# Four quarter-unit subtractions of a Trainium2 decoder kernel, moved from VectorE to GpSimd

## The reference

```python
for i in range(DEPTH):
    h = rms_norm(x, norm_w[i])
    y = nsa_mixer(h, ...) if i % 2 == 0 else hgrn2_mixer(h, ...)
    x = x + y
return rms_norm(x, final_norm)
```

```python
q_raw, f_raw, i_in, z = split(h @ w_in)        # w_in is 1024 x 4096
q = silu(q_raw);  f = lb + (1 - lb) * sigmoid(f_raw);  k = 1 - f
o = recurrence(q, k, log f, i_in)              # 8 heads of 128 x 128 state, decay f
y = (rms_norm_per_head(o) * g_norm * silu(z)) @ w_out
```

## Time and profile before

| | |
|---|---|
| median of 3 runs | 322.13 us (322.1 to 322.6) |
| the profiled execution, whole | 321.99 us |
| its span in the profile | 320.2 us |
| PE busy | 308.6 us, 96% of the span |
| DVE busy | 241.7 us, 75% |
| ACT busy | 183.2 us, 57% |
| POOL busy | 47.2 us, 15% |
| granted TensorE clock | 0.998 of full speed |

### The profile page before, as it was taken

One profiled execution on the slowest core, in us unless ns is written; L12 is line 12 of the kernel. 1 busy time (PEld: TensorE's weight loads), 2 busy tenths in 40 slices (PEclk: granted clock), 3 DMA queues, 4 the chain that ended last, 5 costly groups with the idle time before them and its releaser, 6 DMA issues.

```text
span 320.2 us, 5858 instructions
## 1 busy us (share of the span) xinstructions
PE 308.6 (96%) x2232; PEld 262.3 (82%) x2232; DVE 241.7 (75%) x424; ACT 183.2 (57%) x387; POOL 47.2 (15%) x50
## 2 busy tenths in 40 slices
PE   7999999998999999999999999999999989999992
PEld 4789788866889988887678889999997768889882
DVE  4878987679979888998848825397778997498823
ACT  5886047354794596667446823867273207897423
POOL 1003011031123253446000100000000201103000
PEclk9999999999999999999999999999999999999999
DMA  7999999960192900051270983465914234001011
GB/s 239 394 355 204 259 371 203 313 256 0 41 213 55 211 11 2 0 194 70 66 266 0 333 314 79 186 206 188 332 64 183 81 122 146 3 0 66 2 66 66
DMA packets 28683, 49.33 MB, mean 154 GB/s; under 512 B 3240, under 2 KB 7600, under 8 KB 28656
## 3 DMA queue, kind: packets, MB, share of 16 engines
q1 hardware_dynamic: 25760, 44.30, 44.8%
q10 hardware_dynamic: 2384, 2.63, 4.1%
q0 software_dynamic: 512, 2.03, 1.8%
HBM read 47.90 MB, written 1.05 MB: 153 GB/s over the span
## 4 chain that ended last, share of the span: by engine, by line
PE 78%; DVE 8%; DMA 5%; issue 5%; SPq 1%; ACT 1%; POOL 0%; DVEq 0%; POOLq 0%; ACTq 0%
PE bank L573 72%; DMA raw<-in_nsa 5%; PE bank L749 4%; DVE qk L1141 2%; DVE w_lo L1082 1%; PE bank L672 1%; DVE w_lo L1201 1%; DVE y_hg L1404 1%; PE bank L617 1%; PE bank L816 1%; SPq L555 1%; DVE zT L1271 1%; SPq L552 1%; DVE zT L1272 1%; DVE h_lo L1177 0%
## 5 line engine op out<-in xcount | busy, mean ns | idle before, releaser
L1082 DVE TENSOR_TENSOR w_lo<-raw,w_hi 128x1024 fp32r<-128x1024 f32 (+1 forms) x80 | 87.4, 1141 | 21.2 <-ACT w_hi L846 21.2
L846 ACT ACTIVATE w_hi<-raw 128x1024 fp32r<-128x1024 f32 (+1 forms) x80 | 72.4, 966 | 19.2 <-DMA raw<-in_nsa 15.4
L573 PE MATMUL bank<-w_hi,h_hi 128*128 128x512 f32 x192 | 78.0, 406 | 0.3 <-DVE zT L1272 0.3
L573 PE MATMUL bank<-w_hi,h_lo 128*128 128x512 f32 x192 | 75.2, 392 | 0.2 <-DVE h_lo L1177 0.2
L573 PE MATMUL bank<-w_lo,h_hi 128*128 128x512 f32 x192 | 75.0, 391 | 0.0
L573 PE MATMUL bank<-h_hi,w_hi 128*128 128x256 f32 x224 | 64.7, 289 | 0.0
L573 PE MATMUL bank<-h_hi,w_lo 128*128 128x256 f32 x224 | 63.4, 283 | 0.0
L573 PE MATMUL bank<-h_lo,w_hi 128*128 128x256 f32 x224 | 63.3, 283 | 0.0
L573 PEld LDWEIGHTS bank<-h_hi,w_hi 128*128 128x128 f32 x224 | 42.9, 192 | 0.4
L573 PEld LDWEIGHTS bank<-h_lo,w_hi 128*128 128x128 f32 x224 | 42.9, 192 | 0.4
L573 PEld LDWEIGHTS bank<-w_hi,h_hi 128*128 128x128 f32 x192 | 36.1, 188 | 8.3 <-issue 1.2
(11 more groups left out here) (205 smaller groups left out, 401.9 us busy)
## 6 DMA issues: line engine op xcount, KB each, us to landing
raw<-in_hg SPq DMA_DIRECT2D x16, 1024.0 KB, 7.1
raw<-in_nsa SPq DMA_DIRECT2D x12, 1024.0 KB, 10.4
raw<-in_nsa_out SPq DMA_DIRECT2D x8, 512.0 KB, 8.3
raw<-in_hg_out SPq DMA_DIRECT2D x4, 1024.0 KB, 6.2
raw<-in_nsa SPq DMA_DIRECT2D x8, 256.0 KB, 5.4
w<-in_w1k SPq DMA_DIRECT2D x2, 1024.0 KB, 16.2
w<-in_w1v ACTq DMA_DIRECT2D x2, 1024.0 KB, 14.5
x_res<-in_x SPq DMA_DIRECT2D x4, 256.0 KB, 4.7
```

Of the source, the lines that this page charges most:

```text
L573: return nc.tensor.matmul(o, lhsT, rhs, start=start, stop=stop, skip_group_check=True)
L846: m = nc.scalar.activation(dst, src, ACT.Copy)
L1082: m = V.tensor_tensor(lo, src, hi.bitcast(F32), ALU.subtract)
```

## The change

Of the 80 VectorE subtractions four are given to GpSimd: the last quarter (q = 3) of `V_F1`, `V_Q1`, `V_Z0` and `V_Z1`. GpSimd executes them at the same steps of the list, each after its own `hi_done` wait, and counts them in a semaphore of its own, `lo_pool`. TensorE and SyncE wait on `lo_pool` for these quarters, and `lo_done` is counted without them. Operands, sizes and results are the same.

```diff
+POOL_LO = [(u, NQ - 1) for u in (V_F1, V_Q1, V_Z0, V_Z1)]
+
+def lo_count(u, kk):
+    return split_count(u, kk) - sum(part <= (u, kk // 2) for part in POOL_LO)
...
-                    sp.wait_ge(lo_done, split_count(u - NRAW, KT - 1))
+                    sp.wait_ge(lo_done, lo_count(u - NRAW, KT - 1))
+                    if (u - NRAW, NQ - 1) in POOL_LO:
+                        sp.wait_ge(lo_pool, POOL_LO.index((u - NRAW, NQ - 1)) + 1)
...
             def parts(u, kk):
-                pe.wait_ge(lo_done, split_count(u, kk))
+                if (u, kk // 2) in POOL_LO:
+                    pe.wait_ge(lo_pool, POOL_LO.index((u, kk // 2)) + 1)
+                else:
+                    pe.wait_ge(lo_done, lo_count(u, kk))
...
                 for u, q in SPLIT_LO_AT.get(n, []):
-                    split_lo(u, [q])
+                    if (u, q) not in POOL_LO:
+                        split_lo(u, [q])
...
+                for u, q in SPLIT_LO_AT.get(n, []):
+                    if (u, q) in POOL_LO:
+                        pool.wait_ge(hi_done, split_count(u, 2 * q))
+                        (high, rawp, low), = split_parts(u, q)
+                        GP.tensor_tensor(low, rawp, high.bitcast(F32), ALU.subtract).then_inc(lo_pool, 1)
```

More of the change, by code:

```diff
@@ L350, in program @@
         lo_done = sem("lo_done")
+        lo_pool = sem("lo_pool")
         ident_zero = sem("ident_zero")
```

## The result

| | before | after |
|---|---|---|
| median of the runs | 322.12 us (321.93 to 322.6, 6 runs) | 324.66 us (323.82 to 325.67, 6 runs) |
| ratio, 95% interval | | 1.0077 [1.0061, 1.0094] |
| span of the profiled execution, its mean clock | 320.2 us, 0.998 | 323.4 us, 0.985 |

The account below looks back on a forecast made before the run. TensorE, busy 96% of the span, bounds the kernel, so VectorE time counts only where TensorE waits for it. Median 322.13 plus 1.12 us at `V_Z1`, nothing from the other quarters, gave 323.25 us; range 322.7 to 324.2.

Parts of the forecast that it names:

- D: Length of one GpSimd subtraction on 128 x 1024, taken as 2.45 us, with 2.08 to 2.6 considered.
- The three earlier quarters: At `V_F1`, `V_Q1` and `V_Z0`, moving the subtraction is worth nothing either way, as idle time hides it.
- thin cover at `V_Z0`: Later subtractions use up VectorE's 1.13 us of idle time ahead of L1152; 0 to 0.15 us lost.
- The block on the path: At `V_Z1`, GpSimd delays VectorE's third-quarter subtraction by 2.26 us; less the saved 1.14, TensorE's second wait ends 1.12 later.
- No exclusion: Rival: at `V_Z1` GpSimd's subtraction runs beside VectorE's, saving 1.14 us, to 321.0 us; chance 0.11.
- VectorE first: Rival: `V_Z1`'s third-quarter subtraction precedes GpSimd's, which blocks the decay of 259.1 instead; 0.76 us later, 322.9; chance 0.10.
- TensorE's idle time grows from 1.48 to about 2.6 us: Around `V_Z1`, from 255 to 265 us, TensorE was to lose about 1.1 us of busy time.
- all that follows 264 shifted by one amount: Levels, gate and output behind 264.2 us hang on TensorE and move with it, by 1.12 us.
- The wait of over 2 us: TensorE was to wait over 2 us ahead of the six `V_Z1` matmuls that started at 258.82.

Follow-up runs that it names:

- filled kernels: The full change, and only `V_Z1`'s last quarter on GpSimd, each with eight useless matmuls ahead of the six waiting ones: 323.97 and 323.87 us.
- last-only kernel: Against the full change, only the last quarter of `V_Z1` on GpSimd, the other three back on VectorE: 324.69 us, 1.0081 of before.
- the control: The kernel before with only one TensorE step, `("pa", V_Z0, 1, 0)`, moved ahead of the six waiting matmuls: 325.08 us, 1.0070 of before.

## Why the prediction was right and wrong

- **D, the length of GpSimd's subtraction: right.** 2.41 us undisturbed at 237.63, predicted 2.45. Half of the figure for 2048 columns in the Trainium skill (GPSIMD Engine Reference, Elementwise — side-by-side cycle accounting) gives an estimate of 2.25; the trace is 0.16 above it, and doubling the operation of 512 columns was nearer. The other three take 2.87 to 3.16 because they wait for a VectorE operation first.
- **The three earlier quarters worth nothing: right.** 1.0007 [0.9995, 1.0019] for them alone. The thin cover at `V_Z0` held: L1166 starts at 243.94, less the offset 243.75, predicted 243.7 to 243.9.
- **The block on the path: right.** The order (decay, GpSimd, VectorE's subtraction) is that of the text; the subtraction took 3.37 us, predicted about 3.5, and the chain behind it is 1.02 us later, predicted 1.12. "No exclusion", at 321.0, is refuted by the 3.37. "VectorE first" was not what happened; when it was made to happen, the two executions at full clock lost 0.73 and 0.82 us, near its price of 0.76.
- **The step that failed.** "TensorE's idle time grows from 1.48 to about 2.6 us", and "all that follows 264 shifted by one amount". The wait of over 2 us was forecast and came, but it was priced only at its own length. (The idle time itself grew to 2.07 us and not to 2.6: the second wait, 0.41 us in before and in the filled kernels, is gone inside the slow matmuls.) The text read the clock of 1.00 off the rows of before and carried it over to a kernel in which TensorE stands still for 2.07 us at once. Behind that wait the clock fell to 0.50, and the matmuls that followed cost 2.28 us more in its profile and 0.89 in the last-only kernel's, which is of the lower group; no execution of either came near the 323.1 of the block alone. Nothing in the trace of before could give this price: its waits there of 1.07 and 0.41 us left the clock at 1.00. But that the profile has a column for the clock, and that the change doubles (1.07 to 2.07 us) the longest wait beside the point that sets the end, was reason enough for a rival "the wait costs the clock as well". There was none, and the range of 324.2 ended below the result for this one reason.
- **Only argued.** What decides whether the clock falls is open. By the mean clocks, the kernels with waits of 2.31 and 2.03 us fell in some executions and not in others, those with 2.07 in at least eleven of twelve, the control with 1.22 in ten of twelve, and before, with 1.07 and then 0.41, in none of 58 at 0.991 or less (two are at 0.992). Why the low stretch is twice as long in some profiles is open too. The upper groups of the two filled kernels, at full clock, have no cause that I can show; single executions of before (323.33 and 323.40, clock 0.998) and of the first three alone (323.62, 0.998) also lie 1.2 to 1.3 us above their medians at full clock.

## What to carry to other kernels

Price a lengthened wait of TensorE twice: at its own length, and at the matmuls behind it on half the clock, with a chance for each, and look at the granted clock of the stretch and not only at busy time, which hides a slow clock as work. Work given to GpSimd with SBUF inputs stops VectorE's two-input SBUF operations for its whole length, so look for a stretch where VectorE works out of PSUM: the same quarter cost 2.5 us at one step and gained 1.1 at another. And when executions of a kernel fall into groups, list the mean clock beside each time before any of them is explained.

## What the runs showed of the hardware that I had not expected

- TensorE's clock went from 1.00 to 0.50 behind a wait of 1.22 us (step moved, with and without the change), and stayed there for 3.4 and 6.8 us in which TensorE was busy all the time.
- Behind the same wait of 2.07 us the clock was low from 262.6 to 269.4 us in one profile and from 261.4 to 264.8 in another, and it cost 2.3 and 0.9 us. The two groups of after are 1.7 us apart, and what the runs show to differ between them is the mean clock.
- The schedule before stands close to this edge. Moving one step of TensorE by ten places, to where its data were ready, cost up to 3.8 us.
